# Seven products for all up-projection panels of the gated perceptrons but three

## What is computed

```python
ff = (silu(h @ w_gate) * (h @ w_up)) @ w_down     # 1024 -> 2816 -> 1024, twice in the model
h  = layer_norm(ALPHA * h + ff, g, b)
```

## Time and profile before

| | |
|---|---|
| median of 3 runs | 1964.82 us (1964.78 to 1966.34) |
| the profiled execution, its own time | 1964.29 us |
| its span, first to last instruction | 1962.5 us |
| TensorE (PE) busy | 1928.8 us, 98% of the span |
| DVE, ACT, POOL busy | 57%, 41%, 17% |
| mean granted TensorE clock | 0.995 of full speed |
| gated perceptrons' up panels | about 1060 to 1260 us and 1620 to 1820 us |

### The profile page before, as it was taken

How to read it: one execution, slowest core, us unless ns; L and a number is a source line. 1 busy time by engine, 2 the same in 40 slices (tenths; PEclk the granted TensorE clock), 3 DMA queues, 4 the chain that set the end, 5 groups by cost and what they waited for, 6 DMA issues and landing times.

```text
span 1962.5 us, 29944 instructions
## 1 busy us (share of the span) xinstructions
PE 1928.8 (98%) x12504; PEld 1281.4 (65%) x12504; DVE 1124.7 (57%) x1547; ACT 810.1 (41%) x1313; POOL 339.4 (17%) x355
## 2 busy tenths in 40 slices
PE   8999999999999999999999999999999999999997
PEld 5655655657676654886567666648766586666576
DVE  6666786656477642245767765523565668656224
ACT  6443411445355531133545544312464545444222
POOL 1011111410034320024011511100500124211001
PEclk9999999999999999999999999999999999999999
DMA  7211200232312322322230323323111123232321
GB/s 251 86 65 65 79 29 22 86 129 87 129 64 87 126 99 99 108 108 87 68 120 30 129 87 129 108 93 144 44 65 47 41 86 108 87 129 87 121 94 44
DMA packets 28241, 179.83 MB, mean 92 GB/s; under 512 B 2961, under 2 KB 7185, under 8 KB 7185
## 3 DMA queue, kind: packets, MB, share of 16 engines
q1 hardware_dynamic: 27312, 170.93, 24.5%
q10 hardware_dynamic: 512, 4.94, 0.7%
q0 software_dynamic: 288, 2.10, 0.3%
HBM read 175.86 MB, written 2.10 MB: 91 GB/s over the span
## 4 chain that ended last, share of the span: by engine, by line
PE 67%; DVE 1%; ACT 1%; issue 0%; ACTq 0%; DVEq 0%
PE psum_a L422 17%; PE psum_a L424 17%; PE psum_a L423 17%; PE psum_b L422 4%; PE psum_b L424 4%; PE psum_b L423 4%; PE psum_b L559 2%; PE psum_b L1171 1%; PE psum_a L1125 0%; PE psum_a L1190 0%; PE psum_b L570 0%; PE psum_a L1238 0%; PE psum_a L1245 0%; PE psum_den L1171 0%; PE psum_b L850 0%; PE psum_b L722 0%
## 5 line engine op out<-in xcount | busy, mean ns | idle before, releaser
L2015 DVE SCALAR_TENSOR_TENSOR W_PARTS<-W,W_PARTS 128x2048 f16<-128x2048 f32 x111 | 255.2, 2301 | 306.3 <-ACT W_PARTS L1346 306.2
L1346 ACT ACTIVATE W_PARTS<-W 128x2048 f16<-128x2048 f32 x111 | 211.0, 1904 | 275.0 <-PE psum_a L424 272.7
L422 PE MATMUL psum_a<-U,W_PARTS 128*128 128x512 f16 (+1 forms) x808 | 301.6, 373 | 1.5 <-DVE U L2135 1.5
L423 PE MATMUL psum_a<-U,W_PARTS 128*128 128x512 f16 (+1 forms) x808 | 301.4, 373 | 0.0
L424 PE MATMUL psum_a<-U,W_PARTS 128*128 128x512 f16 (+1 forms) x808 | 301.4, 373 | 0.0
L422 PE MATMUL psum_a<-ARENA,W_PARTS 128*128 128x256 f16 (+1 forms) x860 | 269.1, 313 | 2.3 <-DVE ARENA L2668 2.3
L424 PE MATMUL psum_a<-ARENA,W_PARTS 128*128 128x256 f16 (+1 forms) x860 | 269.0, 313 | 0.0
L423 PE MATMUL psum_a<-ARENA,W_PARTS 128*128 128x256 f16 (+1 forms) x860 | 268.9, 313 | 0.0
L2975 POOL TENSOR_TENSOR ARENA<-ARENA 128x512 f16<-128x512 f32 x76 | 108.0, 1431 | 430.8 <-ACT ARENA L1480 430.7
L424 PEld LDWEIGHTS psum_a<-U,W_PARTS 128*128 128x128 f16 x808 | 79.1, 98 | 90.4
L422 PEld LDWEIGHTS psum_a<-U,W_PARTS 128*128 128x128 f16 x808 | 79.1, 98 | 87.7 <-issue 4.1
(11 more groups left out here) (376 smaller groups left out, 4044.7 us busy)
## 6 DMA issues: line engine op xcount, KB each, us to landing
W<-weights SPq DMA_DIRECT2D x159, 1024.0 KB, 4.8
CON<-const ACTq DMA_DIRECT2D x1, 3071.5 KB, 12.9
X<-x_in SPq DMA_DIRECT2D x4, 256.0 KB, 4.0
X<-x_in SPq DMA_DIRECT2D x1, 1024.0 KB, 8.0
U<-dft POOLq DMA_DIRECT2D x1, 1024.0 KB, 5.8
ARENA<-dft POOLq DMA_DIRECT2D x1, 1024.0 KB, 5.4
U<-mem_in ACTq DMA_DIRECT2D x1, 1024.0 KB, 4.8
y_out<-U SPq DMA_DIRECT2D x2, 512.0 KB, 2.9
```

What stands on the lines that cost most here:

```text
L422: nc.tensor.matmul(out, left(0), right(0), start=first, stop=False, skip_group_check=goes_on)
L423: nc.tensor.matmul(out, left(0), right(1), start=False, stop=False, skip_group_check=goes_on)
L1346: nc.scalar.activation(HOMES[home_of[g]][:, 0, :], W[g % 2][:, :], ACT.Copy, scale=W_SCALE).then_inc(sem("panel_high"), 1)
L2015: nc.vector.scalar_tensor_tensor(out=home[:, 1, :], in0=W[g % 2][:, :], scalar=W_SCALE, in1=home[:, 0, :], op0=ALU.mult, op1=ALU.subtract) ...
```

## The change

The gate panels of groups 2 to 10 become sevens as well, so a gated perceptron has gate 0, up 0 and gate 1 as plain panels and 19 sevens. The order is up 1, gate 2, up 2, gate 3, up 3 and so on. Sevens at odd places (the gates; `second_set`) keep their blocks in the panel buffers `W_PARTS` and use `psum_den` and two `psum_a` banks, those at even places (the ups) keep the old places. `q7` and `q4` of one seven now stand inside the next seven, and `add_part`, `block_sums` and the splits of three neighbouring sevens are interleaved. Silu of a gate is made in place from the added-up tile (`gate_silu`). A tile multiplication that needed `q4` moves to its own step (`finish_21`). The squared-ReLU perceptron keeps its steps. 18 panels change from plain to seven.

```diff
                 if gated:
-                    self.pairs = [(("gate", j), ("up", j)) for j in range(1, groups)]
+                    self.plain, self.sevens = ("gate", 1), [("up", 1)]
+                    for j in range(2, groups):
+                        self.sevens += [("gate", j), ("up", j)]
...
+        ODD_RAW = W_PARTS[:, 0, :].bitcast(F16).rearrange("p (l b k c) -> p l b k c", l=2, b=4, k=4)
+        ODD_SUMS = W_PARTS[:, 1, 0:3 * BLOCK].bitcast(F16).rearrange("p (l b k c) -> p l b k c", l=2, b=3, k=4)
...
+                def seven_panel(at):
...
+                    one_of_seven(at, "q1")
...
+                    one_of_seven(at, "q5")
+                    if M.gated and at:
+                        sixth(at - 1)
+                    one_of_seven(at, "q2")
...
+                    one_of_seven(at, "q6")
+                    if M.gated and at:
+                        seventh(at - 1)
...
+                    one_of_seven(at, "q3")
...
+            def sevens_low(M, src):
+
+                first, second, third = M.sevens[0:3]
+                raw_low(M, first)
+                block_sums(M, first)
+                sums_low(M, first)
+                rest_low(M, first)
+                v_made(M, src, V7)
+                block_sums(M, second)
+                raw_low(M, second)
+                sums_low(M, second)
+                v_low(M, (V7,))
+                v_made(M, src, V4)
+                add_part(M, first, 0)
+                add_part(M, first, 1)
+                v_low(M, (V4,))
+                add_part(M, first, 2)
+                block_sums(M, third)
+                raw_low(M, third)
+                finish_21(M, first)
+                sums_low(M, third)
+                rest_low(M, second)
+                add_part(M, second, 0)
+                finish_gated(M, first)
+                for at in range(2, len(M.sevens)):
+                    key, before, following = M.sevens[at], M.sevens[at - 1], M.sevens[at + 1:at + 2]
+                    add_part(M, before, 1)
+                    for next_one in following:
+                        block_sums(M, next_one)
+                    rest_low(M, key)
+                    add_part(M, before, 2)
+                    for next_one in following:
+                        raw_low(M, next_one)
...
+                    add_part(M, key, 0)
+                    for next_one in following:
+                        sums_low(M, next_one)
+                    if before[0] == "up":
+                        finish_21(M, before)
+                        finish_gated(M, before)
```

More of the change, by code:

```diff
@@ L370, in build, with blocks_view, second_set @@
+        def blocks_view(M, at, l, first, end):
+            if not second_set(M, at):
+                return M.blocks[:, l, first:end]
+            if first in (S1, S2, S4):
+                return ODD_SUMS[:, l, first - S1:end - S1]
+            shift = A11 if first < S1 else A22 - 2
+            return ODD_RAW[:, l, first - shift:end - shift]
+        def second_set(M, at):
+            return M.gated and at % 2 == 1
         NORMS = ("mix", "mem", "x", "ff", "final", "ln_mix0", "ln_ffn0", "ln_mix1", "ln_ffn1")
@@ L1498, in used_panels, with pairs_high @@
                     split(panel_of[M.name, key] + 2)
[L1500 to L1506 removed]
+            def pairs_high(M):
                 before = None
@@ L1534, in mlp @@
                         v_high(M, (V7, V4))
-                        for j in range(1 if M.gated else 2):
+                        for j in range(2):
                             hidden_high(M, j)
-                    if before and not M.gated:
+                    if before:
                         hidden_high(M, plain[1])
@@ L1545, in mlp @@
+            def mlp(M):
+                if not M.gated:
+                    first_tiles(M, 1, 0)
+                split(head_panel(M.norm, 2))
+                for j in range(1 if M.gated else 2):
+                    first_tiles(M, j, 1)
+                v_high(M, (V5, V6))
+                if M.gated:
+                    sevens_high(M)
+                else:
+                    pairs_high(M)
                 used_panels(M, M.down_panels[:-3])
@@ L2082, in v_low, with banks_of @@
                                                    op0=ALU.mult, op1=ALU.subtract).then_inc(sem("v_low"), 1)
+            def banks_of(M, at):
+                if not second_set(M, at):
+                    return psum_b
+                first = A.at[(M.name,) + M.plain + (1,)] + 1
+                return [psum_den] + [A.banks[(first + i) % 4] for i in range(2)]
             def add_part(M, key, i):
-                n, j = M.seven[key], key[1]
-                dest = GF if M.gated else TS
+                n, j, at = M.seven[key], key[1], M.sevens.index(key)
+                dest = GF if M.gated and key[0] == "up" else TS
                 m, half = ((0, 0), (0, 1), (1, 1))[i]
@@ L2284, in used_panels, with pairs_low @@
                     split(panel_of[M.name, key] + 2)
+            def pairs_low(M, src, hidden):
+                before = None
+                for n, (plain, seven) in enumerate(M.pairs):
+                    if before:
+                        add_part(M, before, 1)
+                        add_part(M, before, 2)
+                        block_sums(M, seven)
+                        raw_low(M, seven)
+                        if n == 1:
+                            hidden(M.pairs[0][0][1])
+                        finish(M, before, 0)
+                        sums_low(M, seven)
+                        finish(M, before, 1)
+                        rest_low(M, seven)
+                        split(panel_of[(M.name,) + seven] + 1)
+                    else:
+                        raw_low(M, seven)
+                        block_sums(M, seven)
+                        for j in range(2):
+                            for half in range(2):
+                                hidden(j, half)
+                        sums_low(M, seven)
+                        rest_low(M, seven)
+                        split(panel_of[(M.name,) + seven] + 1)
+                        v_made(M, src, V7)
+                        v_made(M, src, V4)
+                        v_low(M, (V7, V4))
+                    if before:
+                        hidden(plain[1])
+                    add_part(M, seven, 0)
+                    before = seven
+                add_part(M, before, 1)
+                finish(M, before, 0)
+                split(panel_of[(M.name,) + before] + 2)
+                add_part(M, before, 2)
+                finish(M, before, 1)
```

395 lines of the change are left out of this document (256 added, 139 removed).

## The result

The changed kernel takes **1978.26 us** (median of 4 runs, 1976.54 to 1980.48) against 1964.8 us before (4 runs, 1961.86 to 1966.34): a ratio of **1.0072**, 95% interval 1.0056 to 1.0088. It is slower, by 13.5 us between the two medians (14 by the ratio), and 0.7 us under the forecast of 1979. Run again beside the last experiments it gave 1.0073 (1.0060 to 1.0086).

A forecast was written before the change was run, and what follows sets the result against it. PE bounded the kernel before; afterwards DVE and the loads pace the pairs. Each perceptron loses 7.1 + 0.6 + 1.5 + 8 pairs x 1.11 = 18.1 us and saves 10.9, so 14.4 longer for both: 1979.2 us, range 1967 to 1989.

The forecast's parts named there:

- The rate: PE in the pairs: two sevens take 18.32 us against 19.53, saving 10.9 us a perceptron if PE never waits.
- DVE's work and the collisions: Up half of a pair: DVE has 16.5 us of work a pair; two POOL passes each delay a sum 0.84 us.
- The load: Gate half of a pair: DVE sits some 1.1 us waiting for the load, landing 4.8 us after issue.
- what would show it: Signs in the later profile: slow up sums, load wait before gate sums, PE waits, one of some 5 us near 1105.
- The start: Start of each gated perceptron: gate 2's third `add_part` comes at 1110.2, wanted at 1103.1, so PE loses 7.1 us.
- The two rescaling terms: POOL's rescaling passes slow DVE at each perceptron's start: 0.6 us before the late addition, 1.5 in the pair after.
- The sum: Each perceptron loses 18.1 us and saves 10.9: 7.2 us longer, 14.4 for both, giving 1979.2 us.
- rival 3: Loads are slower beside busier engines, 5.1 us each: +8 us, so 1987 us; chance 11%.
- rival 2: Only one of POOL's two passes hits DVE's sums: pair 18.6 us, 1965 us, no change to speak of; chance 10%.
- rival 1: POOL's passes miss DVE's sums: PE's 18.32 us decides the pair, only the start costs, 1956 us; chance 6%.
- Rival 4: Everything is hidden, the start too: 21.8 us less, so 1943 us; chance 3%.

The follow-up runs named there:

- one_input: Changed kernel with POOL's `hidden_low` passes of groups 1 to 9 reading one SBUF input instead of two (low part set to zero); 1964.93 us, 1.0009.
- pool_late: Changed kernel with POOL's two passes of a group held back until DVE finished `rest_low` of the gate panel two groups on; 1967.20 us, 1.0016.
- extra_pass: Changed kernel with POOL making the second `hidden_low` pass of every group from 1 on twice; 1997 us, 1.0161.
- filler: Changed kernel with 39 unread matmuls of 256 columns added in each gated perceptron, right before PE's long wait for gate 2's third `add_part`; 1.0058.
- changed_again: The changed kernel run once more, as yardstick on the same chip; 1.0073.
- all_three: Changed kernel with `rest_low` and `rest_high` ahead in the loop, gate 2's rest early at the start, POOL's rescaling passes late; 1957.05 us, 0.9965.

## Why the prediction was right

**The rate.** PE's saving stands: 18.33 us a pair where nothing holds PE up (one_input), for 18.32 worked out from the earlier trace rows, against 19.53.

**DVE's work and the collisions.** Both POOL passes hit, as forecast: 0.84 and 0.85 us, taken as 0.84 from the earlier trace rows. The Trainium skill (SBUF — State Buffer, "Who interferes with whom") has the two engines contend when GpSimd reads SBUF and DVE has two inputs there, and calls the port that they share an exclusive lock: the trace agrees on who waits and that it goes both ways (POOL at 1.54 and 1.38). It agrees nearly in size too, better than the prediction's estimate of a whole pass of 1.15 us, since a sum can wait only for what is left of POOL's pass. The sum at 1182.70 starts 0.98 us before that pass ends (1182.14 + 1.54 = 1183.68) and takes 0.84 longer than 0.69; in pool_late 0.93 us were left (1209.01 + 2.27 - 1210.35) and it took 0.80 longer; in extra_pass 1.10 (1191.94 + 1.49 - 1192.33) and 0.96. So in three kernels it is the rest of the pass less some 0.14 us. It does not fit where POOL reads one input: in one_input some 1.3 us of POOL's pass are left at 1197.75, and the sum takes only 0.29 longer.

one_input shows that without these 1.7 us PE paces, and extra_pass that a further pass adds 0.96. One count is off, and nothing rests on it: the passes with two inputs in SBUF are 14.1 of DVE's 16.5 us by the earlier trace rows (2 x 6.59 and 0.95 of the finish), not 13.5.

**The load.** 1.10 and 1.17 us of wait where about 1.1 was worked out. The pair measured 19.33 to 19.39 for 19.43, PE's loss 1.0 for 1.11. ACT, costed at nothing with an estimated 12 of 18.3 us, is busy 98.31 of 178 us (55%, 10.7 us of a pair) and makes PE wait once, for 0.6 us.

**Where I had the halves crossed.** In "what would show it" I put the slow sums on the up panels and the wait ahead of the gate's sums. The rows show the reverse: the sums that meet POOL are those of the next gate panel (they stand in the iteration of an up), and the wait is ahead of the next up's. That naming was wrong; the sequence and the numbers were worked out in the right order.

**The start.** The third `add_part` of gate 2 was to come at 1110.2, PE wanting it at 1103.1: 7.1 us, and 0.6 for rescaling. DVE's rows after:

```profile
1103.04 0.69 DVE L2195 TENSOR_TENSOR ARENA<-W 128x512 f32<-128x512 f32 x1 [2.70 <-DMA W<-weights]
...
1107.30 0.41 DVE L2275 SCALAR_TENSOR_TENSOR ARENA<-psum_den,SQ 128x256 f32<-128x256 f32 x1
```

It ends at 1107.71, which is 29.7 us behind PE's first seven, where q4 was due at 22.3: 7.4 us. The forecast of one wait "of some 5 us or more" is the 4.7 in PE's waits; the remainder went in shorter ones ahead of it. Behind it the first perceptron loses 17.9 - 7.4 - 8 x 1.01 = 2.4 us more, where I had 1.5 (a guess between 0 and 3). The two rescaling terms, 0.6 and 1.5, were oversized: moved away, those passes give back 0.24 us up to the addition (4.43 us from the first sum to its end and not 4.67) and 1.05 in all (197.15 to 196.10), not 2.1. The lower clock, which no step of mine had, has at most the 0.7 us that filler won. About 0.9 us of the 2.4 stay open.

**The sum.** The first perceptron loses 197.15 - 179.2 = 17.9 us where the prediction had 18.1, and is 7.0 longer where it had 7.2. Its pairs are 0.8 us under the forecast (8 x 1.01 for 8 x 1.11), the start 0.6 over. In the second it loses 3.0 more, and this is rival 3 in part. Usual loads land in 4.7 us as before, but now and then one takes over 6, and in the new order nothing covers it. The load issued at 1774.59, and DVE's wait for it:

```profile
W<-weights SPq DMA_DIRECT2D x1, 1024.0 KB, 6.1
```

```profile
1780.72 0.69 DVE L2195 TENSOR_TENSOR ARENA<-W 128x512 f32<-128x512 f32 x1 [2.49 <-DMA W<-weights]
```

That wait is 1.4 us longer than the usual one. Two more such loads, issued at 1744 and 1804 us, come ahead of a gate's sums, where DVE usually waits for nothing and now waits 1.17 and 1.09 us. They recur: in changed_again the same three panels (issued at 1745, 1775 and 1805 us) take 6.1 to 6.3 us again, and a fourth at 1837 takes 6.0. In all_three, a load of 7.3 us at 1773.6 leaves no trace: its second perceptron is 187.71 us against 187.80. I forecast loads as they were, and rival 3 a general slowing; it was single ones. The trace of the kernel before has them too (7.2 and 7.3 us, issued at 1660 and 1679 us): the 4.7 to 5.0 of the earlier trace rows were read in the first perceptron alone. Why they are long stays open.

**What of the closeness is luck.** The two stretches of sevens together are 7.0 + 10.1 = 17.1 us longer, where the sum had 14.4, and yet the two spans differ by 1976.9 - 1962.5 = 14.4. The changed kernel reaches its first seven 2.8 us earlier (1077.99 against 1080.81 us), in a part where the two programs do the same work. In the profile before the mean granted clock is 0.72 from 22 to 28 us and from 268 to 274 us, in the changed kernel's it is 1.00 in both; over all these runs the part takes 1078.0 to 1082.1 us. So the mechanism was forecast to within 3 us, and the last 2.7 us of agreement were made by two things that were not in the sum, the long loads and this scatter.

**The rivals.** Those on the collisions came true only where made to. pool_late is rival 2, one pass hitting: its pair is 18.48 us where I had 18.6, and its time 1.0016 where I had no change. one_input is nearest to rival 1, with PE's pace in the pairs; it is level with the kernel before (1.0009) and not 9 us under it. The start there costs what it did, with the slow matmuls, and long loads come on top, so rival 1's 1956 us was too low even on its own terms. Rival 4 needs the start hidden, which nothing here did.

## What to carry to other kernels

A cheaper matmul scheme is paid for on the vector engine: when that goes from 63% to 92% of a stretch, list every pass in order and price each wait and each collision in the pair, since the saving on PE (1.21 us) is lost to items of 1 us each. Then look for the order before giving up the idea: moving one step ahead on two engines took back the whole loss, with the same work. A wait removed shows what stood in the queue behind it, so look for the next one (here ACT's `rest_high` behind a `hidden_high`) before running.

## What the runs showed of the hardware that I had not expected

- After a wait of 4.8 us PE's granted clock was 0.50 for the next 24 matmuls of 256 columns, 0.21 us each against 0.109; with the wait filled by matmuls it stayed at 1.00. After the waits of up to 1 us in the pairs it did not fall.
- A POOL pass of 128x512 with one SBUF input (1.84 us, two in 3.68) holds DVE's two-input pass up by 0.29 and 0.42 us; one with two inputs (1.15 us undisturbed) by 0.80 to 0.96, which is what is left of it when DVE's pass starts, less 0.14 us.
- Most 1 MB loads land in 4.7 us, but single ones took 6.1 (changed) and 7.3 (all_three), and 7.2 in the kernel before (issued at 1660 us), whose second perceptron is as short as its first. Three of the long ones came at the same panels in both profiled executions of the changed kernel.
